# Inference step of a hybrid decoder: the first operands split into a quarter and a rest on two queues, and two chunks of the last residual update given to GpSimd

## What is computed

```python
for i in range(DEPTH):
    mkv_p = mem_kv_proj(mem_prompt, w_mem_kv[i])        # (256, 1024) @ (1024, 512): keys and values of the memory
    hp = rmsnorm(xp, norm_mix_pre[i])
    ...                                                  # token mixer and memory attention give mp
    xp = xp + rmsnorm(mp @ w_out[i], norm_mix_post[i])
    xp = xp + rmsnorm(swiglu_ffn(rmsnorm(xp, norm_ffn_pre[i]), w_ffn_in[i], w_ffn_out[i]), norm_ffn_post[i])
return xp, ...                                           # the same for the 32 sample columns
```

## Time and profile before

| what | value |
|---|---|
| median of 3 runs | 1134.69 us (1133.3 to 1135.32) |
| the profiled execution | 1134.15 us, of which the span from first to last instruction is 1132.5 us |
| PE busy | 1071.6 us, 95% |
| DVE, ACT, POOL busy | 355.7 us (31%), 201.2 us (18%), 243.3 us (21%) |
| mean granted clock of TensorE | 0.981 |
| moved by DMA | 185.21 MB, 164 GB/s over the span |

### The profile page before, as it was taken

How to read it: one execution, slowest core, us unless ns; L and a number is a source line. 1 busy time by engine, 2 the same in 40 slices (tenths; PEclk the granted TensorE clock), 3 DMA queues, 4 the chain that set the end, 5 groups by cost and what they waited for, 6 DMA issues and landing times.

```text
span 1132.5 us, 17040 instructions
## 1 busy us (share of the span) xinstructions
PE 1071.6 (95%) x6364; PEld 786.5 (69%) x6364; DVE 355.7 (31%) x849; ACT 201.2 (18%) x497; POOL 243.3 (21%) x314
## 2 busy tenths in 40 slices
PE   7899999999999999999999999895698999999996
PEld 5666666666777777777776777454676777777774
DVE  4729777532142111100023225885004211110002
ACT  3321000012231000000013223574012100001000
POOL 0706766641001011000000005266300111010000
PEclk9999999999999999999999999998798999999998
DMA  8918443330425656576343226379531533433431
GB/s 337 354 52 264 127 126 112 112 112 14 174 81 186 225 206 254 196 299 223 128 163 131 103 92 198 133 261 331 196 145 47 185 116 145 143 117 113 142 128 67
DMA packets 59407, 185.21 MB, mean 164 GB/s; under 512 B 8641, under 2 KB 39618, under 8 KB 48962
## 3 DMA queue, kind: packets, MB, share of 16 engines
q1 hardware_dynamic: 50882, 164.10, 41.5%
q0 software_dynamic: 6144, 12.59, 3.6%
q10 hardware_dynamic: 2304, 7.47, 1.8%
HBM read 180.36 MB, written 10.02 MB: 168 GB/s over the span
## 4 chain that ended last, share of the span: by engine, by line
PE 88%; issue 4%; DVE 4%; POOLq 1%; DMA 1%; POOL 1%; ACT 1%; DVEq 0%; SPq 0%
PE banks L746 30%; PE banks L512 15%; PE banks L786 15%; PE banks L718 15%; PE banks L539 2%; PE banks L687 1%; POOLq L396 1%; PE banks L585 1%; PE banks L1134 1%; PE banks L700 1%; PE banks L880 1%; PE banks L487 1%; PE banks L728 1%; DMA slabs<-in_w 1%; DVE rstd L1663 1%
## 5 line engine op out<-in xcount | busy, mean ns | idle before, releaser
L746 PE MATMUL banks<-normed,slabs 128*128 128x288 f32 x1408 | 345.1, 408 | 4.6 <-ACT normed L1243 4.6
L746 PEld LDWEIGHTS banks<-normed,slabs 128*128 128x128 f32 x1408 | 269.2, 191 | 80.1 <-issue 5.0
L786 PE MATMUL banks<-hidden,slabs 128*128 128x288 f32 x704 | 171.2, 406 | 1.5 <-issue 1.5
L718 PE MATMUL banks<-arena,phase 128*128 128x384 f32 x512 | 170.6, 490 | 0.0
L786 PEld LDWEIGHTS banks<-hidden,slabs 128*128 128x128 f32 x704 | 133.6, 190 | 39.1 <-issue 2.4
L718 PEld LDWEIGHTS banks<-arena,phase 128*128 128x128 f32 x512 | 95.6, 190 | 63.3 <-issue 0.2
L1558 POOL TENSOR_TENSOR projected<-projected,rstd 128x288 f32<-128x288 f32 x44 | 34.9, 793 | 426.5 <-ACT projected L1310 426.5
L512 PE MATMUL banks<-normed,slabs 128*128 128x288 f32 (+1 forms) x416 | 107.7, 411 | 1.2 <-ACT normed L1243 1.2
L512 PEld LDWEIGHTS banks<-normed,slabs 128*128 128x128 f32 (+1 forms) x416 | 75.5, 187 | 26.2 <-ACT normed L1243 3.2
L1655 DVE TENSOR_TENSOR normed<-normed 128x288 f32<-128x288 f32 x24 | 11.0, 459 | 199.0 <-ACT normed L1303 199.0
L1310 ACT ACTIVATE projected<-projected 128x288 f32<-128x288 f32 x44 | 19.5, 442 | 281.1 <-DVE projected L1702 281.1
(11 more groups left out here) (302 smaller groups left out, 1064.8 us busy)
## 6 DMA issues: line engine op xcount, KB each, us to landing
slabs<-in_wfi SPq DMA_DIRECT2D x44, 1024.0 KB, 4.9
slabs<-in_w SPq DMA_DIRECT2D x24, 1024.0 KB, 5.0
arena<-in_cmp SPq DMA_DIRECT2D x128, 192.0 KB, 2.8
slabs<-in_wfo SPq DMA_DIRECT2D x32, 704.0 KB, 4.0
arena<-in_slck POOLq DMA_DIRECT2D x64, 96.0 KB, 3.1
arena<-in_slck SPq DMA_DIRECT2D x64, 96.0 KB, 3.4
out_win_old<-in_winold SPq DMA_DIRECT2D x8, 762.0 KB, 6.4
arena<-in_slcv SPq DMA_DIRECT2D x48, 96.0 KB, 4.1
```

The costliest lines, as they stand in the source:

```text
L718: ins = nc.tensor.matmul(out.rearrange("p h (g s) -> p h g s", s=8), W1S[:, c, a, j, :], PG[b % 2][:, :, c * 8 + j, :, :].rearrange("p g h ...
L746: return nc.tensor.matmul(BK[2 * (u % SLOTS) + c][:, 0:T], wt[:, k, c * P:c * P + P], Hn[:, k, :], start=(k == 0), stop=(k == KC - 1), ski ...
L786: ins = nc.tensor.matmul(BK[b][:, 0:T], wt[:, k, :], HD[:, 11 * kh + k, :], start=(kh + k == 0), stop=(kh * 11 + k == 21))
```

## The change

At the start the operands of the first product are split at chunk 2 in place of chunk 4: a quarter of 256 KB and a rest of 768 KB, for the memory tokens and for the slab alike. SP issues the two parts of the tokens, ACT, as its first instructions, the two parts of the slab. PE waits for the quarters before its first matmul and for the rests before chunk 2. SP's queue has two transfers fewer ahead of all its others.

At the end DVE makes the last residual update for chunks 0 to 5 alone. POOL waits for the reciprocal (`rs_done`), multiplies chunks 6 and 7 by `RST`, waits for both, and adds both to the residual, counting the new semaphore `last_x_done`. SP's last store waits for that semaphore; the first three are as before.

```diff
-                            if l + s + t == 0 and k == 4:
+                            if l + s + t == 0 and k == 2:
                                 pe.wait_ge(memt_loaded, 16)
                                 slab_ready(pe, n)
...
+            act.dma_start(W_[:, 0:2 * 256], w8_in[0][:, 0:2 * 256]).then_inc(first_half, 16)
+            act.dma_start(W_[:, 2 * 256:SLAB], w8_in[0][:, 2 * 256:SLAB]).then_inc(slab_loaded[0], 16)
             act.wait_ge(prm_loaded, 16)
...
             channel_mixer(1)
 
+            pool.wait_ge(rs_done, 8)
+            for k in (KC - 2, KC - 1):
+                ins = tt(Z[:, k, :], Z[:, k, :], RST[:, :], ALU.mult)
+                if k < KC - 1:
+                    ch.tick(ins)
+                else:
+                    ch.step(ins)
+            for k in (KC - 2, KC - 1):
+                tt(X[:, k, :], X[:, k, :], Z[:, k, :], ALU.add).then_inc(last_x_done, 1)
...
-                for k in range(KC + 1):
-                    if k < KC:
+                for k in range(chunks + 1):
+                    if k < chunks:
                         ch.tick(tt(Z[:, k, :], Z[:, k, :], RST[:, :], ALU.mult))
...
-            post_norm(7)
+            post_norm(7, KC - 2)
...
-            sp.dma_start(M_[:, 0:4 * NMEM], mem_in[:, 0:4 * NMEM]).then_inc(first_half, 16)
-            sp.dma_start(W_[:, 0:4 * 256], w8_in[0][:, 0:4 * 256]).then_inc(first_half, 16)
-            sp.dma_start(M_[:, 4 * NMEM:KC * NMEM], mem_in[:, 4 * NMEM:KC * NMEM]).then_inc(memt_loaded, 16)
-            sp.dma_start(W_[:, 4 * 256:SLAB], w8_in[0][:, 4 * 256:SLAB]).then_inc(slab_loaded[0], 16)
+            sp.dma_start(M_[:, 0:2 * NMEM], mem_in[:, 0:2 * NMEM]).then_inc(first_half, 16)
+            sp.dma_start(M_[:, 2 * NMEM:KC * NMEM], mem_in[:, 2 * NMEM:KC * NMEM]).then_inc(memt_loaded, 16)
...
             for k in range(0, KC, 2):
-                wait_x(sp, 3, k + 1)
+                if k < KC - 2:
+                    wait_x(sp, 3, k + 1)
+                else:
+                    sp.wait_ge(last_x_done, 2)
                 sp.dma_start(y_out[:, k * T:(k + 2) * T], X_[:, k * T:(k + 2) * T]).then_inc(stored, 16)
```

More of the change, by code:

```diff
@@ L340, in trunk_kernel @@
         memkv_stored, state_stored = sem("mem_kv_stored"), sem("state_stored")
+        last_x_done = sem("last_chunks_updated")
         stored, pt_loaded = sem("stored"), sem("page_table_loaded")
@@ L1668, in pre_norm, with post_norm @@
                 inverse_root(norm)
-            def post_norm(norm):
+            def post_norm(norm, chunks=KC):
                 sum_squares(norm, Hn[:, 0, :], [Hn[:, k, :] for k in range(1, KC - 1)])
                 inverse_root(norm)
-                for k in range(KC + 1):
-                    if k < KC:
+                for k in range(chunks + 1):
+                    if k < chunks:
                         ch.tick(tt(Z[:, k, :], Z[:, k, :], RST[:, :], ALU.mult))
                     if k:
-                        ch.sync(but=1 if k < KC else 0)
+                        ch.sync(but=1 if k < chunks else 0)
                         tt(X[:, k - 1, :], X[:, k - 1, :], Z[:, k - 1, :], ALU.add).then_inc(x_done, 1)
```

## The result

The changed kernel takes 1143.51 us (median of 6 runs, 1140.76 to 1148.32), the kernel before in the same measurement 1135.01 us (6 runs, 1133.3 to 1136.13). The ratio is 1.0077, 95% interval 1.0053 to 1.01: slower by 8.5 us. The sign and the two places were forecast; the size (+2.7 us) and the range (up to 1138.6) were not. The profiled execution of after is its slowest, 1148.32 us, with a span of 1146.6 us, 14.1 us over the 1132.5 of before. So the first question is which of these 14.1 us belong to the change.

The account below looks back on a forecast made before the run. The prediction took PE, busy 95% of the span, to bound the kernel, with DVE's last norm and a store at the end. Start +1.5 and end +1.2 gave +2.7 us on 1134.69: 1137.4 us, range 1134.5 to 1138.6.

Parts of the forecast that it names:

- The sign and the two places: Slower, chance 0.49; lost at the start, at PE's new wait at matmul 3, and at the end, on DVE and the stores.
- What bounds the kernel: Whole span: PE busy 95%; a shift of the row sums at 20.27 goes through in full; DVE's last norm ends it.
- five rivals: Early rest 0.25; no DVE/POOL holding at the end 0.10; both 0.06; longer slow start 0.10; POOL part failing, other mishaps 0.04.
- Part 1: Start: the quarters land and PE begins at about 5.0 us, 2.4 us earlier.
- Part 2: Start: PE does two matmuls, then waits at matmul 3 for the rest, landing at 9.31, between 7.3 and 9.96.
- upper end: Start: latest landing taken for the rest of the operands, 9.96 us, against the 9.31 forecast.
- Rival 1: PE's wait at matmul 3: the rest comes early, by 7.8, start costs nothing, end +1.2 us: 1135.9; chance 0.25.
- rival 4: Start: rest at 9.96 or later and a longer slow stretch, +2.8 us, with the end 1138.7; chance 0.10.
- Part 3: Start: ten slow matmuls again after the wait, products end at 21.75 for 20.27: +1.5 us, between −0.3 and +2.8.
- Part 4: End on DVE: four instructions fewer, −1.48, held by POOL, +2.28: net +0.8 us, between −1.48 and +1.7.
- Part 5: Last stores: one more issue on SP's path, +0.38 us, or +0.66 if the two transfers share the engines.
- The sum: Start +1.5 and end +1.2 us: +2.7 us in all, 1137.4 us.

## Why the prediction was right and wrong

**What bounds the kernel** held: the shift of the row sums (+3.5) goes through to 675 us at its full size. What lay at the very end of the span was read too shortly. "1132.1 of 1132.5", the last store's landing against the span, was right for before, and I took it that the program would always end with its last store. The rows of line 178 were there, with a drain of 11.4 us on the very engine that the change was going to wake 92 us after its last work. "POOL is idle there" was taken for free; idle until the end was not the same as free, as this idleness hid the drain. None of the five rivals held this cost. It is 4.6 of the 6.2 us at the end.

**Part 1** (PE begins at about 5.0): wrong, 7.73. The step was to take the landing time of 512 KB issued first, 4.97, for that of two quarters issued together. The quarters' landings were 0.87 + 5.7 for the tokens and 0.87 + 6.8 for the weights: a quarter has as many pieces as a half, one for each partition, and from 3 to 5 us packets, not bytes, are the measure.

**Part 2** (the rest at 9.31): wrong twice. First a miscount. The projection runs over 2 slabs, 2 halves of the rows and 8 chunks, 32 matmuls, and has 64 records: two for each. "Matmul 5" at 9.31 is record 5 and belongs to chunk 2, which was in the first half all along. The first that needs the rest is record 9. The matmuls of before from 7 to 11 us, as one group (ns min/median/max, first and last start):

```profile
L539 PE MATMUL banks<-slabs,mixed x8: 634/634/796, 7.4 to 10.6; 128*128 128x256 f32 x8
```

so record 9 starts at about 11.0, and the row gives no bound below 9.96 for the landing. The prediction's "upper end", 9.96, was the only value that the rows held; the four records of after (and not "two") show the count. Second, "the bytes are the same" again: the rest landed at 11.33, 1.4 us behind 9.96, of which 0.8 us is the pieces (quarter, one queue) and 0.6 the second queue with the earlier issue that goes with it. "DMA engines 91% busy" was read as a full load; the share is of time in which engines have a packet in hand, and at 209 GB/s beside 434 it says nothing of bytes. Rival 1, an earlier rest, went the wrong way; rival 4 ("9.96 or later") had the direction, but its price ended at +2.8 us. Of the page that I named (DMA: Bandwidth & Descriptors, in the Trainium skill, Issuing engines are not separate DMA queues) this case's runs agree in kind: the second queue moved nothing forward, and the 0.6 us that it cost here is beyond what the page states.

**Part 3** (the slow matmuls restart): right in mechanism, and the size came out by luck. After the pause the records are slow again (after, 11.4 to 16 us and 16.7 to 20 us, the same view):

```profile
L540 PE MATMUL banks<-slabs,mixed x11: 634/634/767, 11.5 to 15.9; 128*128 128x256 f32 x11
...
L540 PE MATMUL banks<-slabs,mixed x17: 379/379/551, 16.3 to 19.9; 128*128 128x256 f32 x17
```

Eleven are at 634 ns or more, a twelfth at 551 starts at 16.3, and then they are fast: 5.2 us of slow records, where before had ten in 4.4 us. From profile to profile this stretch varies by more than that, from 3.1 us (halves on two queues) to 6.1 (the start alone). The 44 records take 12.28 us where the forecast had 12.40 for 46: two slow ones more and two records fewer cancel. The windows print a granted clock of 1.00 over these stretches, but that is no reading: the trace holds no level of the clock before 11.9 us in before and 16.6 us in after, which is where the slow records end. So it is their pace (0.43 us apart against 0.216) that shows the slowness. With the true landing in the forecast's own sum, 11.33 + 0.14 + 12.28 = 23.75. The whole miss of the start, 2.0 us, is the landing. The second slab was to be issued 1.1 us earlier and to land as before; it was issued at 5.04 (before 5.25) and landed 12.8 us later, at 17.8 in place of 16.45. It is there when the third product of after begins, at about 20.3 (23.75 − 16×0.216), so this cost nothing.

**Part 4** (DVE −1.48 + 2.28 = +0.8): right, +0.9. The four POOL instructions stretched DVE's records from 0.45 to 1.04 us, each by 0.59 us, 2.4 us in all. By the rule of the SBUF page of the Trainium skill taken to the letter (SBUF — State Buffer, Who interferes with whom) the net was to be +1.7; the trace has about half of it, and the rows of the start had priced it.

**Part 5** (+0.38): the right mechanism, somewhat small. From the first product SP's drain lies 1.7 us later than before (9.96 against 8.2), of which DVE has 0.9; the two late stores have 0.8, above their upper bound, 0.66. As their longest landing is now 2.5 us where it was 2.1, some 0.4 of it may be the two sharing the DMA engines.

**The sum** was +1.5 and +1.2; it is +3.5, +1.7 and 4.6 of drain. What the forecast named as what would overthrow it, "something between 41 and 1120 us moves against the start's shift", did happen in the profiled execution, but it isn't the cause of the miss. Without it both ends give 9.7 us.

## What to carry to other kernels

Before work is put on an engine that is idle at the end, look at what that engine does when it is done: here POOL's closing drain ends 10.6 us after its last instruction, and whatever POOL does within that distance of the end sets the end. Before an early transfer is cut smaller, look at packets per microsecond, not at bytes or at the DMA share: while these are few, as here in the first 5 us, smaller pieces land hardly earlier and all that is behind them lands later. And count the records of one matmul before a record's start is taken as a bound for a transfer.

## What the hardware showed

- POOL's drain at the end of the program ends 10.6 us after POOL's last instruction, whether this was a product of 0.79 us at 1030.9, a memset of 0.1 us, or a sum of 0.9 us; PE's, ACT's and DVE's drain records are 0.5 to 0.8 us long, SP's 7 ns. A memset of 128 numbers cost 2.4 us of span by it.
- From 4 to 5 us the kernels moved 44 to 65 operand packets, of 2 to 8 KB alike, which is 90 to 434 GB/s; from 7 to 8 us before moved 117 packets and 422 GB/s. From 2 to 3 us the large packets were fewer (14 of 8 KB, 60 of 4 KB).
- With the weights on a second issuing queue (ACT beside SP), which also issued their rest 0.9 us earlier, PE's first matmul came 0.6 us later with halves (8.02 against 7.44) and 0.7 us later with quarters (7.73 against 7.06).
- At 682 us, behind a stretch of 106 short matmul records in 4 us, the mean granted clock of the two windows was 0.50 to 0.67 in both profiles of the change, and before has no dip there; it cost 1.7 us. One profile of each kernel can't tell whether a shift of this size comes from the edit: here it stands in four of four profiles with the second queue and in none of seven without, while the medians hardly show it.
